# First expert product of a PEER layer: one 448-column and one 224-column matmul per weight tile, against three of 224 columns

## The reference

```python
q = (xf @ w_q).reshape(n, PEER_HEADS, 2, PEER_DK // 2)
s = jnp.einsum('nhpd,hpkd->nhpk', q, sub_keys)
...            # the 16 best pairs of keys per token and head: eidx, gates g
act = jax.nn.gelu(jnp.einsum('nd,ned->ne', xt, u[it]), approximate=False) * gt
return jnp.einsum('ne,ned->nd', act, v[it])
```

## Time and profile before

| | |
|---|---|
| median of 3 runs | 2077.51 us (2077.25 to 2081.11) |
| profiled execution, span from first to last instruction | 2076.7 us |
| PE busy | 2000.0 us, 96% |
| weight loads (PEld) busy | 1778.1 us, 86% |
| DVE busy | 1534.5 us, 74% |
| ACT busy | 858.4 us, 41% |
| POOL busy | 707.7 us, 34% |
| mean granted TensorE clock | 0.983 |
| first expert product | 680.9 to 1360.4 us |

### The profile page before, as it was taken

One profiled execution on the slowest core, in us unless ns is written; L12 is line 12 of the kernel. 1 busy time (PEld: TensorE's weight loads), 2 busy tenths in 40 slices (PEclk: granted clock), 3 DMA queues, 4 the chain that ended last, 5 costly groups with the idle time before them and its releaser, 6 DMA issues. The chain is left out here.

```text
span 2076.7 us, 29610 instructions
## 1 busy us (share of the span) xinstructions
PE 2000.0 (96%) x11208; PEld 1778.1 (86%) x11208; DVE 1534.5 (74%) x2439; ACT 858.4 (41%) x863; POOL 707.7 (34%) x504
## 2 busy tenths in 40 slices
PE   7999998998799999999999998999999999999997
PEld 6987775997799999999999888988888888888886
DVE  5988755454588788899989897467767777677876
ACT  4340146333333654455454444444343434334333
POOL 2000110220426777577876875010101001123410
PEclk9999998999899999999999999999999999999999
DMA  5463393443244677878877787778999888998984
GB/s 204 162 198 131 121 398 125 151 169 106 83 146 141 230 251 269 290 262 306 274 272 275 273 306 284 283 260 329 351 343 343 326 329 344 359 362 351 379 306 142
DMA packets 101227, 531.28 MB, mean 256 GB/s; under 512 B 19376, under 2 KB 21568, under 8 KB 45792
## 3 DMA queue, kind: packets, MB, share of 16 engines
q1 hardware_dynamic: 71552, 408.93, 55.0%
q0 software_dynamic: 24304, 106.45, 14.0%
q10 hardware_dynamic: 5296, 14.98, 1.9%
HBM read 491.34 MB, written 38.14 MB: 255 GB/s over the span
## 5 line engine op out<-in xcount | busy, mean ns | idle before, releaser
L863 DVE TENSOR_TENSOR wl<-raw,wh 128x2048 fp32r<-128x2048 f32 x310 | 714.5, 2305 | 284.9 <-ACT wh L531 284.5
L531 ACT ACTIVATE wh<-raw 128x2048 fp32r<-128x2048 f32 x310 | 593.3, 1915 | 577.5 <-DMA raw<-in_v 417.1
L1451 PE MATMUL acc<-xhl,wh 128*128 128x448 f32 x2048 | 652.1, 377 | 7.5 <-DVE wl L863 7.4
L1452 PE MATMUL acc<-xhl,wl 128*128 128x224 f32 x2048 | 546.7, 267 | 0.0
L1451 PEld LDWEIGHTS acc<-xhl,wh 128*128 128x128 f32 x2048 | 385.4, 188 | 45.0 <-DVE wl L863 9.7
L1452 PEld LDWEIGHTS acc<-xhl,wl 128*128 128x128 f32 x2048 | 392.7, 192 | 0.0
L1853 POOL DMA_INDIRECT G<-gsum,cell x224 | 344.0, 1536 | 100.2 <-issue 75.2
L1428 PE MATMUL acc<-xhl,wh 128*128 128x288 f32 x768 | 232.5, 303 | 24.7 <-DVE wl L899 14.6
L1429 PE MATMUL acc<-xhl,wh 128*128 128x288 f32 x768 | 229.7, 299 | 0.0
L1430 PE MATMUL acc<-xhl,wl 128*128 128x288 f32 x768 | 228.7, 298 | 0.0
L1428 PEld LDWEIGHTS acc<-xhl,wh 128*128 128x128 f32 x768 | 147.0, 191 | 27.5 <-DVE wl L899 14.6
(11 more groups left out here) (277 smaller groups left out, 2654.5 us busy)
## 6 DMA issues: line engine op xcount, KB each, us to landing
raw<-in_u SPq DMA_DIRECT2D x128, 1024.0 KB, 5.2
raw<-in_v SPq DMA_DIRECT2D x128, 1024.0 KB, 6.0
raw<-in_w_mix SPq DMA_DIRECT2D x28, 1024.0 KB, 5.2
G<-zero SPq DMA_DIRECT2D x16, 1024.0 KB, 14.0
raw<-in_w_out SPq DMA_DIRECT2D x16, 1024.0 KB, 4.9
raw<-in_w_pq SPq DMA_DIRECT2D x16, 1024.0 KB, 4.9
gin<-G SPq DMA_DIRECT2D x32, 512.0 KB, 8.1
h<-hbg ACTq DMA_DIRECT2D x32, 448.0 KB
```

The source lines that it names most:

```text
L531: act.activation(wh[:, n % 4], raw[:, n % 4], ACT.Copy).then_inc(hi_done, 1)
L863: dve.tensor_tensor(wl[:, n % 4], raw[:, n % 4], wh[:, n % 4].bitcast(F32), ALU.subtract).then_inc(lo_done, 1)
L1451: pe.matmul(acc[:, s, 0:2 * NU].rearrange("p (a n) -> p a n", a=2), wh[:, s, j, :], xhl[:, :, j, 0:NU], start=(j == 0), stop=False)
L1452: ins = pe.matmul(acc[:, s, 0:NU], wl[:, s, j, :], xh[:, j, 0:NU], start=False, stop=(j == DT - 1))
```

## The change

Each weight tile gets three matmuls of 224 columns, all summed onto the same 224 columns of the bank. ACT applies gelu straight from the bank to `hbg`, two slots at a time, which frees the banks, and issues the transfer to `h` at the end of the same four slots. The copy to `hsum`, DVE's addition, and the semaphores `half_out` and `gelu_done` are gone; the memory of `hsum` stays as an unused piece.

```diff
             sb(u, "over_al0", [P, 960])
-            hsum = sb(u, "hsum", [P, 2, 2, NU])
+            sb(u, "over_al1", [P, 4 * NU])
...
-            def gelu_of(it_before):
-
-                act.wait_ge(acc_free, slot_no(U0, it_before, 3) + 5)
-                act.activation(hbg[:, 4:8, :], hbg[:, 0:4, :], ACT.Gelu).then_inc(gelu_done, 1)
-                act.wait_ge(gelu_done, it_before + 2)
-                act.dma_start(dr["h"][it_before], hbg[:, 4:8, :]).then_inc(h_out, 16)
-
-            def u_iteration(it, gelu=True, hook=None):
+            def u_iteration(it, hook=None):
                 for s in range(4):
                     hi_next(U0, it, s)
-                    if s == 0 and gelu:
-                        if not (isinstance(it, int) and it == 1):
-                            act.wait_ge(h_out, 16 * (it - 1))
-                        gelu_of(it - 1)
                     if hook:
                         hook(4 * it + s)
                     if s % 2 == 1:
-                        half_evac(2 * it + s // 2)
-
-            def half_evac(q):
-
+                        u_evac(2 * it + s // 2)
+
+            def u_evac(q):
+
+                it, c = q // 2, 2 * (q % 2)
                 act.wait_ge(slot_used, U0 + 2 * q + 2)
-                if q >= 2:
-                    act.wait_ge(acc_free, U0 + 2 * q + 2)
-                c = 2 * (q % 2)
-                act.activation(hsum[:, q % 2], acc[:, c:c + 2, NU:2 * NU], ACT.Copy).then_inc(half_out, 1)
-
-            act.sem_inc(gelu_done, 1)
+                act.wait_ge(acc_free, U0 + 2 * q + 4)
+                to = 4 * (it % 2)
+                act.activation(hbg[:, to + c:to + c + 2, :], acc[:, c:c + 2, 0:NU], ACT.Gelu).then_inc(acc_free, 2)
+                if c == 2:
+                    act.wait_ge(acc_free, U0 + 2 * q + 6)
+                    if it:
+                        act.wait_ge(h_out, 16 * it)
+                    act.dma_start(dr["h"][it], hbg[:, to:to + 4, :]).then_inc(h_out, 16)
...
-            def u_evac(q):
-
-                slot_ready(U0, 0, 2 * q + 1)
-                if q % 2 == 0:
-                    dve.wait_ge(gelu_done, q // 2 + 1)
-                dve.wait_ge(half_out, q + 1)
-                c = 2 * (q % 2)
-                dve.tensor_tensor(hbg[:, c:c + 2, :], acc[:, c:c + 2, 0:NU], hsum[:, q % 2], ALU.add).then_inc(acc_free, 2)
-
...
                 for j in range(DT):
                     if first:
                         pe.wait_ge(split_lo, 3 * DT + CT + j + 1)
-                    pe.matmul(acc[:, s, 0:2 * NU].rearrange("p (a n) -> p a n", a=2), wh[:, s, j, :], xhl[:, :, j, 0:NU], start=(j == 0), stop=False)
+                    pe.matmul(acc[:, s, 0:NU], wh[:, s, j, :], xh[:, j, 0:NU], start=(j == 0), stop=False)
+                    pe.matmul(acc[:, s, 0:NU], wh[:, s, j, :], xl[:, j, 0:NU], start=False, stop=False)
                     ins = pe.matmul(acc[:, s, 0:NU], wl[:, s, j, :], xh[:, j, 0:NU], start=False, stop=(j == DT - 1))
                 ins.then_inc(slot_used, 1)
```

More of the change, by code:

```diff
@@ L363, in build @@
         scattered = [sem("scattered0"), sem("scattered1")]
-        half_out, gelu_done, h_out = sem("half_out"), sem("gelu_done"), sem("h_out")
+        h_out = sem("h_out")
         hg_in, prod_done, ah_done, act_ready = sem("hg_in"), sem("prod_done"), sem("ah_done"), sem("act_ready")
@@ L799, in u_hook @@
                     hst_evac(n % 4)
-            u_iteration(0, gelu=False, hook=u_hook)
+            u_iteration(0, hook=u_hook)
             for it in range(1, 31):
@@ L813, in _ @@
             u_iteration(31, hook=lambda n: act_hi(0, 0) if n == 4 * 31 + 2 else None)
-            act.wait_ge(h_out, 16 * 31)
-            gelu_of(31)
             def v_iteration(i, last, hook=None):
@@ L1320, in _ @@
                 u_extras(n)
-                if n % 2 == 1:
-                    u_evac(n // 2)
             def product(b):
@@ L1400, in _ @@
                     act_lo(0, 0)
-                if s % 2 == 1:
-                    u_evac(62 + s // 2)
             for i in range(NBLK // 2):
```

## The result

The changed kernel takes 2103.4 us, median of 4 runs (2100.3 to 2108.3), against 2079.3 us (2077.3 to 2083.4) for the kernel before on the same chip: a ratio of 1.0119, 95% interval 1.0103 to 1.0136. It is slower by 24 us. The forecast was 13. The direction and the range were right; the size was not.

The account below looks back on a forecast made before the run. PE's pace was taken to bound the first expert product; 11.6 + 0 + 1.4 = 13.0 us on a profiled 2076.7 gave 2089.7, 2090.5 us on the median. The range for 8 in 10 was 2080 to 2104 us.

Parts of the forecast that it names:

- What bounds the kernel: First expert product: PE's pace sets the stage, busy for 665.1 of 679.5 us, with small losses.
- the spacing of the three matmuls: Inside a slot of the first expert product: 109 ns, between 106.7 and 111.8; 0.166 us more a slot, 21.2 over 128.
- signs of being wrong: Spacing under 107 or over 112 ns, slots 82 to row turn changing over 3 us, or second product leaving 226.7 ns.
- Slots 0 to 81: First 82 slots of the first expert product: 13.6 us more, 2 given back from waits for `wl`, 11.6 remain.
- Slots 82 to 115: Stretch up to the second row turn: 5.6 us more vanish into 14.7 us already lost, nothing added.
- Slots 116 to 127: Last slots of the first expert product: 2.0 us more, two parts of 0.3 go into waits, 1.4 remain.
- POOL's queue sets the end: Slots 82 to 115: POOL's own pace to the last pick places the row turn, hiding up to 0.43 us a slot.
- Nothing given back: Rival: POOL's order follows DVE, so no increase is hidden; 21.2 us at 109 ns, 38.4 at 111.8; chance 0.17 including over 112 ns.
- Columns only: Rival: weight loads overlap fully and 224 columns cost 106.7 ns; 2080.6 us; chance 0.11.
- the second `wh` is not loaded again: Rival: each tile has two loads, 309 ns, 7.6 less than now; 2059.9 us; chance 0.03.
- Faster: Rival: the line PE, copy, addition, gelu, `wh` causes PE's losses, so all 21.2 us come back; 2065.3 at 107 ns; chance 0.09.
- ACT and DVE: First expert product: gelu from bank taken as 541 ns, ACT's 45.8 us of waits vanish, DVE 39 us less busy.

Follow-up runs that it names:

- e2: Changed kernel with the matmuls of before (448 and 224 columns per tile), wh.xl half left out of the sum: 2076.7 us against 2077.8, ratio 1.0006.
- e1: Kernel before with three matmuls of 224 columns for 15 of 16 weight tiles, copy and addition kept: 2106.8 us, ratio 1.0146.
- e3: Changed kernel with all three matmuls cut to 192 columns, 32 tokens left out: one run, 2100.87 us.
- e4: Changed kernel with 64 of the 128 weight columns in each load, still 224 moving columns: one run, 2081.92 us.
- e0: Changed kernel again, nothing altered: 2099.96 us against 2077.82 for the kernel before, ratio 1.0110.
- e5: Kernel before with picks 18 and 19 issued later among POOL's gate writes: 2080.2 us, ratio 1.0014.
- e7: Kernel before with 32 more fills on POOL, in its last 32 gate writes: one run, 2078.78 us against 2077.75.
- e12 to e14: Kernel before with picks reading half rows (2075.5 us), DVE's dots over half the columns (2072.1 us), and both (2067.0 us), against 2079.95 us.

## Why the prediction came out as it did

**What bounds the kernel: right.** PE's pace sets the first expert product. e2 shows that lighter ACT and DVE buy nothing with the matmuls of before, e1 that the matmuls alone cost the whole price.

**The step that failed: the spacing of the three matmuls.** The prediction had the right mechanism, a chain of loads of 128 weights with the second `wh` loaded again, and it had both bounds, 106.7 and 111.8 ns. It then took 109, "the in-stage spacing and the middle of both ends". Measured: 111.7, the upper bound to 0.1 ns. The upper bound was the row with most of the same kind in it, the row turns, 32 loads and matmuls in a chain. The transposes, which seemed to speak for less, are of another kind. Another chain of them in the trace of before loads 32 weights each, a quarter:

```profile
1318.27 1.92 PE L1667 MATMUL mis<-cst,hT 128*32 128x128 f32 x16 [1.06 <-ACT xrow L762]
```

(1.92 - 0.27)/15 = 110 ns, as with 128 weights, so their 110 ns is not the price of a load. And one tight pair at a resolution of 10 ns is not a spacing. The lower bound, worked out from columns, did not apply: e3 has the same spacing at 192 columns as at 224, and e4 a smaller one with half the weights. 2.7 ns too little over 48 matmuls is 0.129 us a slot; over the 82 and 12 slots that count it is 12 us, and the miss was 11. The prediction's own sum for 111.8 ns, +25.0 us, is close to what came, +24.1 and in e0 +22.1. None of its signs of being wrong appeared: 111.7 ns is under its 112, and the stretch moved by less than 3 us. They were drawn too wide: 112 ns lets through a spacing that nearly doubles the forecast increase.

The section of the Trainium skill that the prediction cites (TensorE: Matmul & The Clock Gate, Back-to-back issue gap) gives its rule of columns over 2.4 plus 2.5 ns for an isolated matmul, and says that in a stream of loads and matmuls both set the spacing. This case agrees with the second part: the rule gives 95.8 ns for 224 columns, and 111.7 were measured.

**By stretch**, with the span of e0 against that of before. Slots 0 to 81: 82 x 0.294 = 24.1 us more and 2.5 given back by waits (slots 34 and 37 have none now, as foreseen), +21.6; forecast 11.6, or 22.6 at 111.8 ns. Slots 82 to 115: +1.1 (-1.3 in the first profile) where 34 x 0.294 = 10.0 us went in; forecast 0. Slots 116 to 127: +3.5 of matmuls, -0.7 at the wait after slot 119, -2.6 because the row turn ran at full clock, +0.2 in all; forecast 1.4, without the clock. Sum 22.9, and the median of e0 is 22.1 above that of before. That the turn found the full clock was not foreseen: without it the time would have been 2.6 us longer.

**"POOL's queue sets the end": the size held, the cause did not.** The 14.7 us of losses took up 9 to 11 us of matmul time, and the stretch kept its length, as forecast. But a last pick that went out 2.9 us earlier brought nothing (e5), and 11.5 us more work on POOL did not delay it (e7). The losses go when the dots and the rows' transfers are lightened (e12 to e14). The chain of waits showed truly that a row's transfer came last; that POOL's queue made it late was read into it. DVE's 161 of 187 us and the DMA share of 0.82 stood in the earlier trace rows and were not weighed against it. That the size held is in part luck: the argument for it was wrong.

**Rivals.** "Nothing given back" is out: slots 82 to 115 took 10.0 us of matmul time and grew by 1.1; its 38.4 us at 111.8 ns compare with 24.1 and 22.1 measured. "Columns only" and "the second `wh` is not loaded again" are refuted by the spacing and by the 2048 loads of line 1429. "Faster" is refuted by e2: ACT's 45.8 us of waiting for the addition delayed nothing that PE needed, by more than the 1.7 us that the interval of e2 leaves.

**ACT and DVE** went as said: gelu from the bank 545 ns (541 taken), no wait for the addition, DVE lighter by 33.6 us (39 forecast). Taken as worth only the 2 us near slots 34 and 37; e2 measures nothing, e1 leaves room for up to some 7 us beside the slower matmuls.

No version that was tried beats the kernel before with the same output.

## What to carry to other kernels

Splitting one wide matmul in two with the same weights adds a load, and where the columns are fewer than a load of 128 weights takes (here 224 at 111.7 ns), the load is the price; the copies and additions that it saves count only if their engine holds up the weights. To price such a chain take the longest run of the same kind in the trace, not the middle between it and a formula, and check that a row is of that kind: one that costs the same with a quarter of the weights is not. And before a loss is credited as cover, ask which of several loads makes it: here it was at least two at once, and it covered some 10 us of 38.

## What the runs showed of the hardware

**Feeding gaps on TensorE.** In the profile of the changed kernel slot 5 took 6.1 us longer than its neighbours. The timeline of TensorE there:

```profile
707.94 0.26 PE L1430 MATMUL acc<-xhl,wl 128*128 128x224 f32 x1 [0.25 <-issue]
708.04 0.30 PE L1428 MATMUL acc<-xhl,wh 128*128 128x224 f32 x1
708.17 0.28 PE L1429 MATMUL acc<-xhl,wh 128*128 128x224 f32 x1
708.69 0.26 PE L1430 MATMUL acc<-xhl,wl 128*128 128x224 f32 x1 [0.24 <-issue]
...
710.95 0.35 PE L1428 MATMUL acc<-xhl,wh 128*128 128x224 f32 x1 [0.47 <-issue]
711.14 0.27 PE L1429 MATMUL acc<-xhl,wh 128*128 128x224 f32 x1
711.69 0.27 PE L1430 MATMUL acc<-xhl,wl 128*128 128x224 f32 x1 [0.27 <-issue]
```

Matmuls come in small groups some 0.75 us apart, with idle time that no semaphore ends ("issue"). Right behind it the granted clock falls (windows of the same kernel):

```profile
706.80:713.80 7.00, 4.49 (x27) 3.19 (x25) 6.17 (x15) 2.40 (x2) 5.47 (x6) 1.00 0.49 195
713.80:717.20 3.40, 3.35 (x15) 3.15 (x15) 1.84 (x13) 0.00 (x0) 2.79 (x3) 0.52 0.43 104
```

At 0.52, close to the lower level of 1.2 GHz, the matmuls start some 213 ns apart (714.15, 714.36, 714.58 us in the timeline), about twice the 111.7. e0 shows neither gap nor low clock in this place. What starved PE's queue was not tried, and stays open.

**What a matmul costs beside its columns.** With 64 weights the 224 columns cost 102.9 ns, 93.3 ns of columns at 2.4 GHz and 9.6 more, where 288 and 512 columns carry 13.3 more each. So the addition of 13.3 that the prediction carried over does not hold for 224 columns with 64 weights. Whether the columns or the weights make the difference was not tried.
